# Chunk inverses of a two-way RWKV-7 scan: all products in four quarters of the array, second products instead of transposes, and a new order

## The reference

```python
def rwkv7_scan(r, w, k, v, kk, a):
    def step(state, inp):
        r_t, w_t, k_t, v_t, kk_t, a_t = inp
        sa = jnp.einsum('bhvk,bhk->bhv', state, -kk_t)
        state = (state * w_t[:, :, None, :] + sa[..., None] * (kk_t * a_t)[:, :, None, :]
                 + v_t[..., None] * k_t[:, :, None, :])
        return state, jnp.einsum('bhvk,bhk->bhv', state, r_t)
```

## Time and profile before

| | us |
|---|---|
| Median of 3 runs | 2788.41 (2787.0 to 2788.66) |
| Profiled execution, its own time | 2786.51 |
| Span of the profiled execution | 2784.7 |
| PE busy | 2673.3 (96%) |
| DVE busy | 1480.6 (53%) |
| ACT busy | 1221.0 (44%) |
| POOL busy | 377.7 (14%) |

### The profile page before, as it was taken

How to read it: one execution, slowest core, us unless ns; L and a number is a source line. 1 busy time by engine, 2 the same in 40 slices (tenths; PEclk the granted TensorE clock), 3 DMA queues, 4 the chain that set the end, 5 groups by cost and what they waited for, 6 DMA issues and landing times. The chain is left out here.

```text
span 2784.7 us, 52246 instructions
## 1 busy us (share of the span) xinstructions
PE 2673.3 (96%) x22520; PEld 2130.9 (77%) x22520; DVE 1480.6 (53%) x2363; ACT 1221.0 (44%) x2089; POOL 377.7 (14%) x320
## 2 busy tenths in 40 slices
PE   8999999999999999999999999799898988999999
PEld 6887667788888888886588888677677766788887
DVE  3536874733453333445754243696778785743343
ACT  4334763632243222324743232475566765542332
POOL 0023650000000000001200000000453543000000
PEclk9999999999999999999999999899999999999999
DMA  5222002233223223232223223222000002322231
GB/s 186 97 76 92 1 24 91 78 135 107 105 91 106 90 100 105 99 120 72 72 105 106 91 91 106 91 82 86 10 10 8 8 7 66 107 100 104 91 106 61
DMA packets 38820, 228.55 MB, mean 82 GB/s; under 512 B 4368, under 2 KB 8464, under 8 KB 15040
## 3 DMA queue, kind: packets, MB, share of 16 engines
q1 hardware_dynamic: 32576, 201.34, 20.9%
q0 software_dynamic: 6016, 23.87, 2.5%
HBM read 220.93 MB, written 4.26 MB: 81 GB/s over the span
## 5 line engine op out<-in xcount | busy, mean ns | idle before, releaser
L496 DVE TENSOR_TENSOR weights_lo<-ring,weights_hi 128x1024 fp32r<-128x1024 f32 x347 | 427.9, 1234 | 669.6 <-ACT weights_hi L489 664.5
L489 ACT ACTIVATE weights_hi<-ring 128x1024 fp32r<-128x1024 f32 x346 | 363.8, 1053 | 500.8 <-PE bank L713 280.7
L545 PE MATMUL bank<-h_hi,weights_hi 128*128 128x512 f32 x384 | 150.1, 391 | 0.0
L711 PE MATMUL bank<-weights_hi,mlp_p_hi 128*128 128x512 f32 x384 | 149.6, 390 | 0.0
L546 PE MATMUL bank<-h_lo,weights_hi 128*128 128x512 f32 x384 | 149.5, 389 | 0.0
L713 PE MATMUL bank<-weights_hi,mlp_p_lo 128*128 128x512 f32 x384 | 149.4, 389 | 0.0
L712 PE MATMUL bank<-weights_lo,mlp_p_hi 128*128 128x512 f32 x384 | 149.4, 389 | 0.0
L547 PE MATMUL bank<-h_hi,weights_lo 128*128 128x512 f32 x384 | 149.4, 389 | 0.0
L3197 POOL TENSOR_TENSOR scan_b<-scan_a,scan_c 128x512 f32<-128x512 f32 x96 | 124.7, 1316 | 133.7 <-DVE scan_a L3171 111.0
L545 PE MATMUL bank<-mlp_h_hi,weights_hi 128*128 128x512 f32 x336 | 130.7, 389 | 0.0
L546 PE MATMUL bank<-mlp_h_lo,weights_hi 128*128 128x512 f32 x336 | 130.7, 389 | 0.0
(11 more groups left out here) (819 smaller groups left out, 6914.2 us busy)
## 6 DMA issues: line engine op xcount, KB each, us to landing
ring<-in_w_m SPq DMA_DIRECT2D x64, 1024.0 KB, 4.8
ring<-in_w_mb SPq DMA_DIRECT2D x24, 1024.0 KB, 4.7
ring<-in_w_fi SPq DMA_DIRECT2D x22, 1024.0 KB, 4.8
ring<-in_w_fo SPq DMA_DIRECT2D x10, 1024.0 KB, 4.8
ring<-in_w_a SPq DMA_DIRECT2D x7, 1024.0 KB, 4.8
attn_bias<-scratch POOLq DMA_DIRECT2D x16, 448.0 KB, 4.7
ring<-in_w_rg SPq DMA_DIRECT2D x5, 1024.0 KB, 4.9
ring<-in_w_v SPq DMA_DIRECT2D x4, 1024.0 KB, 11.0
```

What stands on the lines that cost most here:

```text
L489: act.e.activation(halves(g, s)[0], raw, ACT.Copy).then_inc(*act.up("act_unit_high", ("high", s)))
L496: lane.e.tensor_tensor(lo, raw, hi.bitcast(F32), ALU.subtract).then_inc(*lane.up(f"{lane.name}_unit_low", ("low", s)))
L545: pe.e.matmul(ps[:, :], hi, xh, start=k == 0, stop=False, skip_group_check=True)
L711: pe.e.matmul(ps[:, :], xh, hi, start=k == 0, stop=False, skip_group_check=True)
```

## The change

A matrix's place gets two bits, `p` (the parity of its chunk, or the half that holds it) and `h` (its head). `pe_items` replaces the other helpers for the inverse: each of its 32 products goes from a half named by one bit to a half named by another, and each group uses all four quarters. Levels 0 and 1 and the last one did so before only in two quarters.

A new group "lower" makes the pieces of level 0 ahead of the products, from half of the columns. DVE drains it through a mask into `T0`, and POOL builds `X` of level 0 from it and the unit matrix in steps of 128x256 elements, four per block; two POOL steps of 128x512 for the mask and two for the sum are gone. `XT` of a level is no more turned from `X` by transposes, but is a second product of `Y` and the older `XT` ("turned"), with operands swapped. `ORDER` is written anew for all engines.

```diff
+    R.T0 = R.LM[0].rearrange("p a t -> p (a t)")[:, 0:512].rearrange("p (d n j t) -> p d n j t", d=2, n=4, j=2)
...
-def pe_to_pairs(g, pe, key, left, right):
-
-    banks = [bank(g, pe, key + (h,)) for h in range(2)]
-    for u in range(2 * NCH):
-        for h in range(2):
-            m = pe_quarter(pe, block(banks[h], u // 2), left[:, u, :], right[:, u, :], h, u % 2)
+def bit(name, p, h):
+
+    return {"p": p, "h": h, "x": p ^ h, "n": 1 - h}[name]
+
+
+AWAY = ("x", "h", "x", "h", "x", "n")
+
+
+def index_bit(level):
+
+    return AWAY[level - 1] if level else "p"
+
+
+def pe_items(g, pe, key, left, right, frm, to):
+
+    banks = [bank(g, pe, key + (j,)) for j in range(2)]
+    for q in range(NCH):
+        for p in range(2):
+            for h in range(2):
+                f = bit(frm, p, h)
+                m = pe_quarter(pe, block(banks[f], q), left(q, p, h), right(q, p, h), f, bit(to, p, h))
...
+ORDER = {'pe': 'mmamtammahrarmamaratamhamamahrmtamammamahmamatamamamaramaama', 'act': 'tttthtrrrrmmthrthmmhhtmtmhhmmhmmammmmmhrmhhhmmmmmmhm', 'dve': 'mmmmmmamammamhataammaahaamamttrrttaammharhahahammathhahamamhamhaaahh', 'pool': 'rmmmmrmmmmtmmmtmmtmhhhhma'}
...
+    for event in ("bb", "minus_kk"):
+        pe.wait_ge(g.at(event, b))
+    banks = [bank(g, pe, ("lower", b, h)) for h in range(2)]
+    for q in range(NCH):
+        for p in range(2):
+            d, c = q // 4, q % 4 * 2 + p
+            for h in range(2):
+                m = pe_quarter(pe, banks[h][:, q * CH // 2:(q + 1) * CH // 2], AR[:, d, c, 0, :], chunks(R.BB[:, d, :])[:, c, d::2], h, p)
+    m.then_inc(*pe.up("pe_products", ("filled", ("lower", b, 0)), ("filled", ("lower", b, 1))))
+    yield
...
-        ps = bank(g, pe, ("x", b, 0, d))
-        pe.wait_ge(g.at("xt", b, 0, d))
-        for c in range(NCH):
-            m = pe_heads(pe, ps[:, c * CH:(c + 1) * CH], XT[:, 8 * d + c, :], R.eye)
-        m.then_inc(*pe.up("pe_inverse", ("filled", ("x", b, 0, d))))
-        yield
-    for name, left, right in (("y", R.LM[1], R.X), ("x", XT, R.Y)):
-        for d in range(2):
-            if name == "y":
-                pe.wait_ge(g.at("masked", b, 1, d))
-                pe.wait_ge(g.at("x", b, 0, d))
-            else:
-                pe.wait_ge(g.at("y", b, 1, d))
-            ps = bank(g, pe, (name, b, 1, d))
-            for u in range(8 * d, 8 * d + 8):
-                m = pe_heads(pe, ps[:, u % 8 * CH:(u % 8 + 1) * CH], left[:, u, :], right[:, u, :])
-            m.then_inc(*pe.up("pe_inverse", ("filled", (name, b, 1, d))))
-            yield
-    for level in range(2, 6):
+        pe.wait_ge(g.at("x0", b, d))
+    pe_items(g, pe, ("xt", b, 0), item(R.X, "h"), lambda q, p, h: R.eye, "p", AWAY[0])
+    yield
+    def y(level):
         for j in range(2):
             pe.wait_ge(g.at("masked", b, level, j))
-            pe.wait_ge(g.at("x", b, level - 1, j))
-        pe_to_heads(g, pe, ("y", b, level), R.LM[level % 2], lambda n: R.X[:, n, :])
+            if level > 1:
+                pe.wait_ge(g.at("x", b, level - 1, j))
+        pe_items(g, pe, ("y", b, level), item(R.LM[level % 2], "h"), item(R.X, index_bit(level - 1) if level > 1 else "h"),
+                 "p", AWAY[level - 1])
+    def y_and_turned(level):
+        for j in range(2):
+            pe.wait_ge(g.at("y", b, level, j))
+            pe.wait_ge(g.at("xt", b, level - 1, j))
+        return item(R.Y, "p"), item(XT, index_bit(level - 1))
+    def x(level):
+        right, left = y_and_turned(level)
+        pe_items(g, pe, ("x", b, level), left, right, AWAY[level - 1], "p")
+    def turned(level):
+        left, right = y_and_turned(level)
+        pe_items(g, pe, ("xt", b, level), left, right, AWAY[level - 1], AWAY[level])
+    y(1)
+    yield
+    x(1)
+    yield
+    for level in range(2, 6):
+        turned(level - 1)
         yield
-        pe_turned_pairs(g, pe, ("xt", b, level - 1), R.X)
+        y(level)
         yield
         if level == 3:
@@ -3115,22 +3134,15 @@
                 pe.wait_ge(g.at("masked_products", b, j))
             pe_to_heads(g, pe, ("g1", b), R.LK[:, 1], lambda n: R.TV[o][:, n % 8, :], cross=1)
             yield
-        for j in range(2):
-            pe.wait_ge(g.at("y", b, level, j))
-            pe.wait_ge(g.at("xt", b, level - 1, j))
         if level < 5:
-            pe_to_pairs(g, pe, ("x", b, level), XT, R.Y)
+            x(level)
         else:
-            pe_last_turned(g, pe, ("xt", b, level), R.Y, XT)
+            turned(level)
         yield
...
+        key = ("lower", b, j)
+        if b:
+            dve.wait_ge(g.at("filled", ("y", b - 1, 4, 0)))
+        ps = filled(g, dve, key)[:, 0:256].rearrange("p (d n t) -> p d n t", d=2, n=4)
+        mask = R.lm[:, :, 0, 0:CH // 2].unsqueeze(2).broadcast_to((P, 2, 4, CH // 2))
+        dve.e.tensor_tensor(R.T0[:, :, :, j, :], ps, mask, ALU.mult).then_inc(
+            *dve.up("dve_middle", ("lower", b), ("drained", key)))
+        yield
...
+    def eye(first):
+        return R.eye[:, first::2].unsqueeze(1).broadcast_to((P, NCH, CH // 2))
+    if b:
+        pool.wait_ge(g.at("filled", ("y", b - 1, 5, 0)))
     for d in range(2):
-        u = slice(8 * d, 8 * d + 8)
-        pool.wait_ge(g.at("masked_first", b, d))
-        if b:
-            for j in range(2):
-                pool.wait_ge(g.at("filled", ("y", b - 1, 5, j)))
-        masked(0, d)
+        u = R.X[:, 8 * d:8 * d + 8, :]
+        pool.e.tensor_copy(u[:, :, 1 - d::2], eye(1 - d)).then_inc(*pool.up("pool_middle"))
         yield
-        pool.wait_ge(pool.newest)
-        if b >= 2:
-            pool.wait_ge(g.at("advanced", b - 2))
-        pool.e.tensor_tensor(R.XT[o][:, u, :], R.LM[0][:, u, :], R.eye.unsqueeze(1).broadcast_to((P, NCH, CH)), ALU.add).then_inc(
-            *pool.up("pool_middle", ("xt", b, 0, d)))
+        pool.wait_ge(g.at("lower", b))
+        pool.e.tensor_tensor(u[:, :, d::2], R.T0[:, d].rearrange("p n j t -> p (n j) t"), eye(d), ALU.add).then_inc(
+            *pool.up("pool_middle", ("x0", b, d)))
```

More of the change, by code:

```diff
@@ L3129, in act_middle @@
     R, o = g.R, b % 2
-    def whole(name, dst, d, level):
-        key = (name, b, level, d)
-        drain_copy(g, act, key, dst[:, 8 * d:8 * d + 8, :], packed(filled(g, act, key)[:, :]), key)
     def both(key, place):
@@ L3142, in act_middle @@
         act.wait_ge(g.at("advanced", b - 2))
-    for level in range(2):
-        for d in range(2):
-            whole("x", R.X, d, level)
-            yield
-    for level in range(1, 6):
-        if 1 < level < 5:
+    for level in range(6):
+        if 0 < level < 5:
             yield from both(("x", b, level), lambda j: by_two(R.X, j))
-        yield from both(("xt", b, level), lambda j: R.XT[o][:, 8 * j:8 * j + 8, :])
+        yield from both(("xt", b, level), lambda j: by_two(R.XT[o], j))
         if level == 2:
@@ L3175, in dve_middle @@
                 yield
-    for d in range(2):
-        ps = packed(filled(g, dve, ("y", b, 1, d))[:, :])
-        dve.e.tensor_tensor(R.Y[:, 8 * d:8 * d + 8, :], ps, R.eye.unsqueeze(1).broadcast_to((P, NCH, CH)), ALU.add).then_inc(
-            *dve.up("dve_middle", ("y", b, 1, d), ("drained", ("y", b, 1, d))))
-        yield
-    for level in range(2, 6):
+    for level in range(1, 6):
         for j in range(2):
@@ L3253, in pe_advance @@
         for d, c, h, n in heads:
-            m = pe_quarter(pe, answer[h], XT[:, 8 * d + c, :], R.U[:, d, :] if i else G1[:, 8 * d + c, :], 1 - h, c % 2,
+            m = pe_quarter(pe, answer[h], item(XT, AWAY[4])(4 * d + c // 2, c % 2, h), R.U[:, d, :] if i else G1[:, 8 * d + c, :], 1 - h, c % 2,
                            start=i == 0, stop=False)
@@ L3932, in _bucket, with lv_first @@
     return np.where(rel > 0, nb, 0) + np.where(n < me, n, np.minimum(large, nb - 1))
+def lv_first(t, s, d):
+    return t == 2 * s[:, 0:CH // 2] + 1 - d
 def _constants():
@@ L3956, in _constants @@
     c["eyes"] = np.tile(np.concatenate([eye, eye - 1.0 / CH], 1), (2, 1)).astype(f)
+    for d, ms in enumerate(lv):
+        ms[0] = np.tile(np.concatenate([lv_first(s, t, d), np.zeros((CH, CH // 2))], 1), (2, 1))
     c["levels"] = np.stack([np.stack(ms, 1) for ms in lv], 1).astype(f).reshape(P, -1)
```

10 lines of the change are left out of this document (7 added, 3 removed).

## The result

The changed kernel took 2838.76 us (median of 5 runs, 2836.72 to 2842.44), against 2788.41 for the kernel before (5 runs, 2783.31 to 2788.66). The ratio is 1.0185, with a 95% interval of 1.0174 to 1.0195. It is slower by 50 us where 8 less were forecast.

A forecast was written before the change was run, and what follows sets the result against it. PE was taken to be bound by its instruction supply. Five steady periods -3.7, last -3.7, first +2.6 and entry -3.5 give -8.3 us from 2786.51, 2778.2; plus 1.9 for the median, 2780 us, range 2755 to 2803.

The forecast's parts named there:

- rival C: Chance 0.25: in the scan, instruction supply is worse than 3.75 us per packet; at 4.1, 18 us slower, 2806 us.
- p: Interval between packets of PE instructions in the scan, taken as 3.75 us, the mean before without a stall.
- What bounds the scan, and the packets: Scan: PE runs just behind the supply of its instructions; 198 instruction packets on queue 8, 18 more than before.
- One of them can be fetched during the thin one: period = 10.2 + 10.2 p: Steady period: 2.1 packets in a thin part of 10.2 us; of 11.2 dense ones one is prefetched; 48.5 us.
- PE work, 41.6 us per period: Steady period: four-quarter products save 3.9 us, the "lower" group costs 0.8; without gaps, 41.6 us of work.
- Waits: Steady period: the recurrence waits 2.1 us instead of 2.8, the products 0.6; together 2.7 us.
- Steady period: Scan's five steady periods: 49.3 us each against 50.04 on average, together 3.7 us less.
- First period and entry: First period, without a tail: 47.4 us against 44.86, +2.6; entry stretch before the first recurrence: -3.5 us.
- A late packet, 0.8 us per period: Beginning of the dense part: a packet late behind SP's in_rk loads costs 2.9 us, counted as 0.8 per period.
- A: Chance 0.13: supply keeps up, 3.4 us per packet or less; steady period 44.9 us, 39 less in all, 2749 us.
- D: Chance 0.12: supply keeps up, but some 11 recurrence steps may each wait 0.2 us more for DVE; 2766 us.
- E: Chance 0.08: cross-quarter products are no faster with these operands, so nothing is saved; 2790 us.

The follow-up runs named there:

- e14: Kernel before, with x of levels 2 to 4 made by 8 transposes of Y instead of 32 products (only time counts): 2778.61 us, ratio 0.9971.
- e9: Kernel before, with SP's loads of in_rk for blocks 2 to 7 cut from 128 partitions to 16: 2786.3 us, ratio 0.9999.
- e10: Changed kernel, with SP's loads of in_rk for blocks 2 to 7 cut from 128 partitions to 16: 2837.29 us, 1.0177 of the kernel before.
- e8: Kernel before, with only the inverse's last product in four quarters instead of two, no instruction more: 2781.19 us, ratio 0.9985.
- e12: Changed kernel, with the turned products of levels 0 to 4 as 8 transposes each (only time counts): 2800.11 us, 1.005 of the kernel before.
- e1: Kernel before, plus two bursts of unread products at the scan's start, 1024 with 64 columns, then 512 with 128: 2873.16 us.
- e5: Four quarters everywhere and "lower" in front, X turned by transposes, steps in the old order: 2820.3 us, 1.0118 of the kernel before.
- e13: Kernel before, plus 40 groups of 64 products (each fifth 80) at the scan's start, each answered by a DVE copy: 2951.32 us.

## Why the prediction was wrong

The outcome is rival C by its mechanism, supply that binds harder than 3.75, which had a chance of 0.25; it lies beyond C's price (2806) and the range's end (2803), in part since C kept the formula that failed and raised only p. Point by point:

- **What bounds the scan, and the packets**: right. 198 packets were forecast and counted; p = 3.75 was taken and 3.68 measured in the burst. The stalls on issue in the cut period end 2.3 to 2.6 us after a packet, as forecast (2.3).
- **"One of them can be fetched during the thin one: period = 10.2 + 10.2 p"**: this step failed. In the cut period no packet arrived before PE had begun the one ahead of it, and PE stalls for 1.24 us as soon as the thin part is over. So nothing is saved, all 11.2 dense packets have to be paid, and the formula is 10.2 + 11.2 p: 52.2 us at 3.75, 3.75 more than the 48.5 that it gave.
- **p itself**: mis-sized for the dense part of the scan. Three thin packets take 14.63 us, 4.88 each, as forecast (10.2 for 2.1). The ten others take 39.63 (3.73 + 19.33 + 3.82 + 3.97 + 3.70 + 5.08), 3.96 each. With 3.96 the formula gives 54.6, and this period, marked as in the stretches, took 54.58. What lifts the mean over 3.68 is in part work (PE is busy 16.77 of the 19.33 us) and in part the packet of 5.08 us, with 1.1 us of waits for DVE and its successor arriving 2.7 us after its beginning where 0.8 to 1.5 is usual in the dense part; why that one came late stays open. A fast packet can't make up for a slow one, since nothing is stored.
- **"That is the mean that before kept up without a stall"**: this ground for p was near the rate of the burst, and hid that before paid too, as e14 shows with its 8.4 us.
- **PE work, 41.6 us per period**: measured 42.7 where the clock was full. "lower" was taken at 0.8 us and its 64 records take 1.09 us and more, as much as with 64 columns moving: the price of 1.05 that was weighed was the true one. In the three other periods the clock adds 2 to 3 us of busy time. The forecast had no term for the clock.
- **Waits**: 2.7 us forecast. In the five periods those for other engines come to 15.7 us, 3.1 each; right. Issue, forecast at 4 or more, is 37.5 us, 7.5 each.
- **Steady period**: 49.3 forecast, 55.1 measured: +1.1 work, some +1.5 clock as the mean over five, +0.4 waits, +2.5 issue (7.5 against the 5.0 left in 49.3 after work and waits); 0.3 lies in gaps too short for these views.
- **First period and entry**: +2.6 forecast, +13.4 measured; it has no tail, so its 1705 records lie denser, and 10 gaps on issue sum to 12.5 us. The entry was to give 3.5 and cost 5.8: with 1409 records instead of 1086 PE is busy 2.2 us longer, the waits for ACT fell from 7.2 to 3.1 us, but issue came with 3.1, those for DVE rose from 1.7 to 5.5, and the clock was 0.93.
- **A late packet, 0.8 us per period**: not the loads' doing, by e9 and e10. The packet came late behind one on which PE worked for 6.74 us.
- **Rivals**: A and D are out, since issue is 61.9 us. E is out: x64 records of y and x take 1.1 us at full clock, and e8 gains.

Open stays why the clock falls. It is 1.00 in every stretch read of before and of e14 (1.0 us of issue), and under 1.00 in some of after and of e12 (20.5 us of issue). Stalls on issue alone need not do it: in the burst of e1, from 1975.92 to 2023.78, PE is busy 27.19 of 47.86 us, with a stall in every packet, at a clock of 1.00; only behind that is it 0.51, from 2024.2 to 2027.7. Nor is much issue needed: e5, with 10.6 us of it but 69 us of waits for DVE and ACT, has 0.98 over the scan. Not shown either is which steps of the new order carry the 13 us that remain at equal count.

## What to carry to other kernels

Count the instructions of a stretch beside its busy time: here 256 PE instructions are delivered per 3.68 us, so work cut into 64-column products that take 2.1 us per 256 starves, and replacing 8 transposes by 32 products of equal busy time at full clock cost 8 to 11 ns per instruction, the clock's part included. Look for idle time on "issue" in mid-group before adding any, and price packets one by one, not by the mean of a stretch: here a thin part left nothing for the dense part behind it. An order written out by hand belongs to its instructions: test the two together and apart.

## What the runs showed of the hardware

- PE had two packets of 256 instructions at hand (e1: 253 records without a gap, then a gap after every 128) and got a new one each 3.68 us; with semaphore waits of 0.32 and 0.78 us in the starved packets it was 3.82 and 3.64 (e13).
- In the scan of after each packet arrived at least 0.6 us after PE had begun the one before it, in the thin part too (46 packets, 2080 to 2268), and in before a packet that took PE 6.84 us put the next arrival off to 6.6 us (2181.6 to 2188.2).
- "lower", 32 fp32 products of a 64x64 load with 32 columns moving, takes 1.09 us, in e5 1.11 and once 1.25, no less than with 64 columns (1.05 to 1.16).
- The granted clock fell to 1.2 GHz for a few us at a time in the starved scan (0.50 from 2180.0 to 2183.5), where in the scan of before it is 1.00 throughout.
